# Decoder step on one core: samples in two groups of four with streamed keys, query tiles in another order

## What is computed

```
s_c = qg . kc ;  p_c = masked_softmax(s_c)          # compressed blocks
score = sum of p_c over the head group, per block of 64 keys
_, idx = top_k(score, 16)                           # selected blocks
s_s = qg . k_sel ;  p_s = masked_softmax(s_s)       # keys of the selected blocks
s_w = qg . kw ;     p_w = masked_softmax(s_w)       # window of 512 keys
o = g0 * (p_c . vc) + g1 * (p_s . v_sel) + g2 * (p_w . vw)
```

## Time and profile before

| | us |
|---|---|
| median of 3 runs | 1167.39 |
| lowest and highest | 1166.18, 1168.58 |
| profiled execution | 1169.66 |
| its span | 1167.9 |
| granted TensorE clock over the span | 0.993 |

### The profile page before, as it was taken

How to read it: one execution, slowest core, us unless ns; L and a number is a source line. 1 busy time by engine, 2 the same in 40 slices (tenths; PEclk the granted TensorE clock), 3 DMA queues, 4 the chain that set the end, 5 groups by cost and what they waited for, 6 DMA issues and landing times.

```text
span 1167.9 us, 17973 instructions
## 1 busy us (share of the span) xinstructions
PE 1125.9 (96%) x7124; PEld 926.1 (79%) x7124; DVE 749.5 (64%) x1375; ACT 386.4 (33%) x822; POOL 360.5 (31%) x364
## 2 busy tenths in 40 slices
PE   6999999999999998999999999899999999998997
PEld 6888999999988855565656465688799999997884
DVE  3677889999974588665555556565655730266745
ACT  3202111123233666756555556401112121353000
POOL 3544520000003687573626345300022221317000
PEclk9999999999999999999999999999999999999999
DMA  7752512343220200231222211732131111041321
GB/s 234 241 164 108 181 36 55 90 170 109 51 41 1 95 25 1 74 116 66 90 92 73 109 35 75 179 127 72 43 112 36 54 36 44 17 145 72 127 90 45
DMA packets 81468, 103.18 MB, mean 88 GB/s; under 512 B 21632, under 2 KB 64776, under 8 KB 81311
## 3 DMA queue, kind: packets, MB, share of 16 engines
q1 hardware_dynamic: 69737, 67.41, 18.8%
q0 software_dynamic: 9472, 33.56, 8.3%
q10 hardware_dynamic: 2182, 1.16, 0.4%
HBM read 90.42 MB, written 16.64 MB: 92 GB/s over the span
## 4 chain that ended last, share of the span: by engine, by line
PE 85%; DVE 5%; DMA 3%; POOL 2%; ACT 2%; issue 2%; SPq 0%; DVEq 0%; ACTq 0%
PE PS L697 24%; PE PS L1682 16%; PE PS L1860 15%; PE PS L1222 6%; PE PS L1208 6%; PE PS L1097 6%; PE PS L685 3%; PE PS L1135 2%; PE PS L1140 2%; DMA WRAW<-in_w_in_even 2%; PE PS L1181 1%; DVE ACC L557 1%; PE PS L1840 1%; DMA WOR<-in_w_out_even 1%; DVE XL L2034 1%
## 5 line engine op out<-in xcount | busy, mean ns | idle before, releaser
L604 DVE SCALAR_TENSOR_TENSOR Y<-U,SM,Y 128x1024 f32<-128x1024 f32 x120 | 147.9, 1293 | 0.3
L697 PE MATMUL PS<-XH,WH 128*128 128x352 f32 (+1 forms) x648 | 147.0, 331 | 0.0
L697 PE MATMUL PS<-XL,WH 128*128 128x352 f32 (+1 forms) x648 | 144.1, 327 | 0.0
L697 PE MATMUL PS<-XH,WL 128*128 128x352 f32 (+1 forms) x648 | 143.3, 325 | 0.0
L697 PEld LDWEIGHTS PS<-XH,WH 128*128 128x128 f32 (+1 forms) x648 | 107.9, 186 | 2.7
L697 PEld LDWEIGHTS PS<-XH,WL 128*128 128x128 f32 (+1 forms) x648 | 108.2, 185 | 1.4
L697 PEld LDWEIGHTS PS<-XL,WH 128*128 128x128 f32 (+1 forms) x648 | 108.0, 186 | 1.4
L1967 POOL TENSOR_TENSOR WL<-WRAW,WH 128x1024 fp32r<-128x1024 f32 x14 | 37.8, 2701 | 217.8 <-ACT WH L1912 217.8
L557 DVE SCALAR_TENSOR_TENSOR ACC<-PS,SM,ACC 128x508 f32<-128x508 f32 x124 | 86.9, 742 | 25.2 <-PE PS L685 23.1
L288 POOL TENSOR_TENSOR WL<-WRAW,WH 128x1024 fp32r<-128x1024 f32 x12 | 28.7, 2390 | 233.1 <-ACT WH L361 233.1
L1682 PE MATMUL PS<-WOH,XH 128*128 128x512 f32 (+1 forms) x288 | 92.2, 402 | 6.1 <-DVE GT L2029 3.1
(11 more groups left out here) (315 smaller groups left out, 2099.6 us busy)
## 6 DMA issues: line engine op xcount, KB each, us to landing
WRAW<-in_w_in_even SPq DMA_DIRECT2D x16, 512.0 KB, 3.9
WRAW<-in_w_in_odd SPq DMA_DIRECT2D x16, 512.0 KB, 4.0
XIN<-in_x_prompt SPq DMA_DIRECT2D x8, 512.0 KB, 13.4
WRAW<-in_w_in_even SPq DMA_DIRECT2D x16, 256.0 KB, 3.7
TM<-in_state_win_kv SPq DMA_DIRECT2D x8, 512.0 KB, 8.8
XR<-in_x_prompt SPq DMA_DIRECT2D x8, 512.0 KB, 3.6
layer_out<-R SPq DMA_DIRECT2D x8, 512.0 KB, 2.6
XR<-layer_out SPq DMA_DIRECT2D x8, 512.0 KB, 3.4
```

The lines of the kernel that those rows point to most:

```text
L604: v.scalar_tensor_tensor(dst, src, CWT[:, i, t:t + 1], dst, ALU.mult, ALU.add).then_inc(s_cv, 1)
L697: ins = pe.matmul(PS[0:mcols, 3 * slot + c, 0:CH], w[:, slot, kk, 0:mcols], x[:, kk, c * CH:(c + 1) * CH], start=(kk == 0 and n == 0), sto ...
```

## The change

1. **Two groups of four samples** instead of four groups of two. A group takes all 128 partitions. RING, of the same size, has room for 2 quarters of 4 samples. Quarters are streamed: keys 0 and 1 are gathered, quarter 2 when the last key turn of quarter 0 is done, quarter 3 likewise behind quarter 1. The products run in 6 parts: quarters 2 and 3, which are there, then the window of samples 2 and 3 of the group and the new tokens, then quarters 0 and 1, gathered a second time (behind parts 0 and 1), then the window of samples 0 and 1, loaded a second time. So there are 6 gathers of four samples per group, 48 DMAs instead of 32, and 12 window loads instead of 8.
2. The window scores of samples 0 and 1 come first in a group, those of 2 and 3 behind quarter 2. They are still scored two at a time (`scw`).
3. Score blocks of the cached keys hold four samples (four strips of 32 columns, 4 KTS tiles). Turns of probabilities are of 128 by 128, five fills of four and one of two. Turned probabilities lie in four places (`turned`).
4. The planner's numbers: a gather of four is 5000 ns, key turns are due 6000 ns after it; parts 3 and 4 of the products likewise. `RANK_LAG`, the distance between ranks, goes from 200 to 1000 ns. DVE's priority goes from PRMOQXHW to PRMOQHXW.
5. Query tiles in the order 3, 2, 1, 0, 4 to 7.
6. SP loads the output weights behind parts 3 and 4 of the second group; the loads of windows wait by `sp_windows_again`.

The diff, cut to its core:

```diff
-            sp_windows(sp, range(2))
+            sp_windows(sp, 0)
-        UNITS = [(qt, gp, br) for qt in (2, 1, 0, 3, 4, 5, 6, 7) for gp in range(2) for br in (SELBR, WINB, CMPB)]
+        UNITS = [(qt, gp, br) for qt in (3, 2, 1, 0, 4, 5, 6, 7) for gp in range(2) for br in (SELBR, WINB, CMPB)]
-        RING = at("RING", [P, 4, 2, 1024], F32, 126720)
-        KTS = at("KTS", [P, 2, 512], F32, 114048)
+        RING = at("RING", [P, 2, 4, 1024], F32, 126720)
+        KTS = [at(f"KTS{i}", [P, 512], F32, o) for i, o in enumerate((114048, 116096, 101376, 103424))]
-        PV_PARTS = 5
+        PV_PARTS = 6
-        RANK_LAG = 200
+        RANK_LAG = 1000
-        for i in range(2):
-            step("POOL", "X", ("gather", 0, i), 2500)
+        step("POOL", "X", ("gather", 0, 0), 5000)
         step("POOL", "X", ("prep",), 3300)
-        for i in range(2, 4):
-            step("POOL", "X", ("gather", 0, i), 2500, ("H", 3))
+        step("POOL", "X", ("gather", 0, 1), 5000, ("H", 3))
...
+        for a in range(2):
+            four = range(4 * a, 4 * a + 4)
+
+            def key_tile(b, i):
+                fill(("kt", b, i), 520, ("late", ("gather", a, i), 6000) if i < 4 else None)
+                take("ACT", ("kt", b, i), 600, ("rank", 1, 5))
+
+            def window_scores(pair):
+                for b in four[2 * pair:2 * pair + 2]:
+                    key_tile(b, 4)
+                fill(("scw", a, pair), 1000)
+                take("DVE", ("scw", a, pair), 920)
+
+            window_scores(0)
+            for i in range(4):
+                for b in four:
+                    key_tile(b, i)
+                if i < 2:
+                    step("POOL", "X", ("gather", a, i + 2), 5000, ("kt", four[3], i))
+                fill(("sc", a, i), 1100)
+                take("DVE", ("sc", a, i), 770)
+                if i == 2:
+                    window_scores(1)
...
+            for i in range(6):
+                fill(("pt", a, i), 550 if i < 5 else 250, ("sscale", a, i // 4))
+                take("ACT", ("pt", a, i), 600)
             for k in range(PV_PARTS):
+                fill(("pv", a, k), (1150, 950, 1400, 950, 950, 950)[k], ("late", ("gather", a, k + 1), 6000) if k in (3, 4) else None)
                 bank7[0] = None
+                if k < 2:
+                    step("POOL", "X", ("gather", a, 4 + k), 5000, ("pv", a, k))
+                if k in (3, 4) and a == 0:
+                    step("POOL", "X", ("gather", 1, k - 3), 5000, ("pv", a, k))
...
-        URGENT = {"PE": "SXTVY", "DVE": "PRMOQXHW", "ACT": "PXEW", "POOL": "CXAW"}
+        URGENT = {"PE": "SXTVY", "DVE": "PRMOQHXW", "ACT": "PXEW", "POOL": "CXAW"}
...
+                    b0 = 4 * x[1] + (2 * x[2] if x[0] == "scw" else 0)
+                    for b in range(b0, b0 + (2 if x[0] == "scw" else 4)):
+                        ins = pe.matmul(PS[rows_of(b), 7, :], QBD[:, b, :], KTS[b % 4][:, :], start=True, stop=True)
...
+                    if part in (3, 4):
+                        pe.wait_ge(s_ring[part - 3], 64 * (3 * a + 3))
+                    if part == 5:
+                        for i in range(2):
+                            pe.wait_ge(s_wc[i], 16 * (3 * a + 3))
+                    four = range(4 * a, 4 * a + 4)
+                    quarter = {0: 2, 1: 3, 3: 0, 4: 1}.get(part)
...
+        def sp_windows_again(sp):
+            for a in range(2):
+                sp.wait_ge(s_xf, bank7_filled(("kt", 4 * a + 1, 4)))
+                sp_windows(sp, 2 * a + 1)
+                sp.wait_ge(s_pvq, 5 * a + 3)
+                sp_windows(sp, 2 * a)
+                if a == 0:
+                    sp.wait_ge(s_pvb, 1)
+                    sp_windows(sp, 2)
...
-                        sp.wait_ge(s_pvq, 14 + kk // 2)
+                        sp.wait_ge(s_pvq, 9 + kk // 2)
-                sp.wait_ge(s_pvq, 16)
-            sp_windows(sp, range(2, DB))
+            sp_windows_again(sp)
```

More of the change, by code:

```diff
@@ L995, in program @@
                      ("late", ("rank", a, n - 1) if n else ("rank", 0, 5), RANK_LAG) if a or n else None)
[L996 to L1005, removed]
+        for a in range(2):
[18 more added lines that the diff above has]
+                    window_scores(1)
+            fill(("new", a), 500)
+            take("DVE", ("new", a), 550)
+            step("DVE", "X", ("low", a), 330)
@@ L1006, in program @@
             for k in range(3):
-                step("ACT", "X", ("sexp", gi, k), 1100 if k < 2 else 920, ("low", gi))
-            step("DVE", "X", ("srec", gi), 400, ("sexp", gi, 2))
+                step("ACT", "X", ("sexp", a, k), 1100 if k < 2 else 920, ("low", a))
+            step("DVE", "X", ("srec", a), 400, ("sexp", a, 2))
             for k in range(2):
[L1010 to L1013, removed]
+                step("POOL", "X", ("sscale", a, k), 810 if k else 2080, ("srec", a))
@@ L1019, in program @@
[L1019 to L1022, removed]
+                if k < 2:
+                    step("POOL", "X", ("gather", a, 4 + k), 5000, ("pv", a, k))
+                if k in (3, 4) and a == 0:
+                    step("POOL", "X", ("gather", 1, k - 3), 5000, ("pv", a, k))
+            take("DVE", ("pv", a, PV_PARTS - 1), 250)
+            fill(("ot", a), 200)
+            take("DVE", ("ot", a), 450)
@@ new lines, in sample @@
+                    quarter = {0: 2, 1: 3, 3: 0, 4: 1}.get(part)
+                    terms = [(22, b) for b in four] if part == 0 else []
+                    if quarter is not None:
+                        terms += [(n, b) for n in range(4 * quarter, 4 * quarter + 4) for b in four]
+                    elif part == 2:
+                        terms += [(n, b) for n in range(16, 20) for b in four[2:]] + [(n, b) for n in (20, 21) for b in four]
+                    else:
+                        terms += [(n, b) for n in range(16, 20) for b in four[:2]]
@@ new lines, in sample @@
+                    for n, b in terms:
+                        c0 = 32 * (b % 4)
+                        if n < 16:
+                            v0 = n % 4 * 256 + P
+                            w = RING[:, n // 4 % 2, b % 4, v0:v0 + P]
+                        elif n < 20:
+                            w = window(b)[:, n - 16, P:256]
+                        if n < 20:
+                            p = turned(n, 1)[:, 0, c0:c0 + 32]
+                        elif n < 22:
+                            v0 = 384 + 256 * (n - 20)
+                            p, w = PTN[:, n - 20, c0:c0 + 32], TM[0:NSAMP, 8, v0:v0 + P]
+                        else:
+                            p, w = PTC[0:NCS, b // 4, rows_of(b)], VCN[0:NCS, b, :]
+                        ins = pe.matmul(PS[rows_of(b), 7, 0:P], p, w, start=(n == 22), stop=(n == (19 if b in four[:2] else 7)))
@@ L1186, in sample @@
+                    ins.then_inc(s_pvb if part == PV_PARTS - 1 else s_pvq, 1)
                 elif x[0] == "ot":
@@ L1356, in sample @@
                 elif x[0] == "srec":
[L1357 removed]
                     v.wait_ge(s_eex, 3 * x[1] + 3)
[L1359 to L1361 removed]
+                    link(v.tensor_tensor(EDN[:, 2:3], EDN[:, 2:3], EDN2[:, :], ALU.add))
+                    v.reciprocal(ERC[:, 2:4], EDN[:, 2:4]).then_inc(s_ern, 1)
+                elif x[0] == "take":
```

175 lines of the change are left out of this document (76 added, 99 removed).

## The result

The changed kernel takes 1154.38 us (median of 4 runs, 1153.95 to 1155.27), beside 1166.99 us for the kernel before on the same chip: a ratio of 0.9891, with a 95% interval of 0.9877 to 0.9905. The profiled execution took 1155.27 us with a span of 1153.5, against 1169.66 and 1167.9.

A forecast was written before the change was run, and what follows sets the result against it. The prediction took a full PE to bound the middle of the attention stage. Work minus 16.8, start minus 3, window plus 7.7 and late loads plus 2 gave minus 10.1 us: 1157.3 us from 1167.4, range 1148 to 1169.

The forecast's parts named there:

- Scores and products: Sample blocks on PE: four strips run at once, so score blocks save 7.9 us and value products 8.4 us.
- Rival (c): Sample blocks on PE: four strips don't run at once, products and scores cost as now, 1174 us; chance 0.03.
- Turns: Turns of probabilities on PE: from 7.0 us to twice 6.5 us a group, minus 0.5 us.
- rival (d): Middle of attention: PE not quite full, half of 16.8 us becomes waiting for DVE or POOL, 1166 us; chance 0.15.
- The window wait: Second group's first window load: PE stands 6 us, then a low clock costs 1.7 us, together plus 7.7.
- Late loads: Twelve fills in attention wait for loads asked for shortly before: plus 2 us for all, ends 0 and 20.
- Rival (a): PE's in-order waits for twelve late loads add up; gain gone at 12 us, 1175 us at 20; chance 0.07.
- The start: Start of attention: tile 3 first and wider-spaced ranks feed PE better, minus 3 us, ends minus 8 and plus 5.
- The chain: Serial sample work beside the prompt: starts near 468 us, ends at 683, 24 us to spare, so not the bound.
- rival (b): The serial sample chain becomes the bound, setting the end from 24 us late; 1173 us at 40 late; chance 0.05.
- The end: End of attention: the stage ends near 721 us and everything behind it shifts alike.

The follow-up runs named there:

- second pair: The changed kernel and the kernel before, both run again unchanged on another chip: ratio 0.9900; the kernel before took 1164.29 us in a single execution.
- tiles_2103: The changed kernel with only the old query tile order 2, 1, 0, 3 put back: 1169.71 us, 1.0019 times the kernel before.
- group_only: The changed kernel with old tile order, old rank distance and old DVE priority, keeping the grouping of four: 1179.86 us, 1.0025 times the kernel before on a slower chip.
- before_again: The kernel before, unchanged, profiled on another chip that turned out like the first: 1164.29 us, a single execution.
- old_ranks: The changed kernel with the old rank distance and ranks ahead of XL put back, tile 3 still first: 1175.00 us, 1.0077 times the kernel before.
- window_later: The changed kernel with the second group's first window scores moved behind quarter 0: 1177.08 us, 1.0004 times the kernel before on a slower chip.
- scores_twice: The changed kernel with every sample score matmul issued twice, same result: 1173.70 us, 0.9968 times the kernel before on a slower chip.

## Why the prediction was right, and where it was not

The forecast was 1157.3 us, the measurement 1154.38, and the mechanism forecast, less work on a full PE, is what the traces show. Point by point:

**Scores and products (minus 7.9, minus 8.4).** Measured by starts: minus 7.7 and minus 8.5. That four strips run at once was read from one block of another kind, and held to the hundredth: 0.99 us a block, 0.25 a term. Rival (c) falls. The Trainium skill ("TensorE: Matmul & The Clock Gate", Part 3, The mechanism) has LDWEIGHTS overlap matmuls in flight only where the row groups differ; the eight records of a term share theirs and still go in 0.25 us, so here the measurement decides against it.

**Turns (minus 0.5).** Turns and new scores together gave minus 1.6. With what the prompt's blocks gained from new neighbours, which the sum did not have, the work fell by 19.0 instead of 16.8.

**PE is full (rival (d)).** It falls: PE's waits for DVE, ACT and POOL in the stage are 8.8 us before and 8.9 after (8.4 and 9.1 in the second pair), where (d) had them grow by 8, and doubled scores show in the time.

**The window wait (plus 7.7).** It came where it was named, near the middle, and the low clock behind it too. It was 2.7 us by the wait, plus 1.7 for 3.4 us of lower clock: some 4.5, and 4.0 in the second pair (2.3 and 1.7). PE was ready for the key turn 2.7 us after the load's issue at 579.29, close to the 2.5 forecast. But the load landed after 5.2 us, not 8.8, and sooner than the shortest in the earlier trace rows, 6.7. This is the term that was too large.

**Late loads (plus 2).** 2.2 us of waits for RING against 0.2 before, with the gathers landing in 4.4 to 9.7 us, median 5.7. Rival (a) falls for this kernel; in tiles_2103 it is half true, 5.6 us.

**The start (minus 3).** Minus 3.3 in the first pair, plus 1.2 in the second. The size was a guess and no run supports it; with the lower clock taken off as above, it is minus 1.4 and minus 2.4.

**The chain (start 468, end 683).** It started at 476.6 and ended at 693.3. Its own length, 216.7 us, was forecast at 215; only its start was off. The ranks and XL alone bring it to 468.4 (tiles_2103), as forecast, against 459.1 in group_only; the new tile order, which the working did not count here, adds the other 8. The chain was not the bound, and rival (b) falls. But between its end and the stage's there were 20.7 us, where the forecast had 38, of which the output weights take 14.

**The end (stage near 721, all behind it moves alike).** The stage ended at 714, 17.4 us earlier. But what lies behind grew by 2.9 us, a step that failed. PE's waits for WOL are 3.0 us as before, but in one piece:

```profile
728.18 1.22 PE L1730 MATMUL PS<-WOH,XH 128*128 128x512 f32 x2 [2.96 <-POOL WOL L1714]
```

In the kernel before they were two pieces of 1.7 and 1.3 with no lower clock behind them. Here the clock is at its lower level for 3.4 us from 728 and 6.8 us from 1042, 3.4 us more lost behind the stage than before.

**The sum in the first pair.** Work minus 19.0, loss plus 3.0 (window 4.5, late loads 2.0, start minus 3.3, and minus 0.2 that has no name), behind the stage plus 2.9: minus 13.1. The stage also began 1.5 us earlier, which the change does not explain, since before_again begins there too; with it the span's 14.4 are accounted for to 0.2. That minus 10.1 came so near is partly luck: the window was 3.2 us too large, the work 2.2 too small, and the growth behind the stage was not in the sum.

**What the working lacked.** It put the change down as terms that add up, and gave the plan none. The order of all engines is planned anew for every edit, and kernels that had the same work removed came out between 0.989 and 1.008. tiles_2103, old_ranks and window_later are each one to three lines from the changed kernel; two lie at or above the upper end of the range and all above the kernel before or level with it. What undid the 19 us in them is named above (projection ahead of value blocks, late loads, lower clock, and on slower chips PE's late counts), but not priced: no run took one away without bringing another. None of it could be read from the trace of before. So the sum was right about the work and right by half an accident about the loss: 6.7 forecast (7.7, 2 and minus 3), 3.0 and 7.4 in the two pairs.

## What to carry to other kernels

Cost work on a full, in-order engine from start to start, and use one block of the trace that already has the new shape: that gave two terms to within 0.2 us. But where a planner makes the order, an edit is also a new draw of the order, here worth 1 to 2%: look at the new order before believing a sum (what now stands ahead of the last blocks, how many gathers go in a row, which load is asked for last), and test an edit in more than one order before crediting it. Do not credit the removal of a wait with the wait's length: in three kernels here the wait went and the gain expected of it did not come, though on other chips than the changed kernel's. And where a wait is put down to nobody, look at what its semaphore counts before guessing.

## What was not expected of the hardware

Two kinds of chip. The kernel before took 1167 us on two and 1176 to 1177 on three. A part goes with the granted clock, 0.997 on the even chip and 0.990 to 0.992 on the slower ones (medians of its executions). At 0.993 to 0.994 its span is 1165.2 to 1168.0 on the first and the even chip and 1171.7 to 1174.0 on the slower ones, so some 6 us remain. Behind the stage the profiles of both kinds agree (436 to 440 us), so the difference is likely to lie in the attention stage. Only the slower chips show counts of PE that reach ACT and DVE late: stops of 0.7 to 3.0 us beside short rows of gathers, 12.8 us beside eight in a row. The kernel before has such a row of eight, so a part of the time that the slower chips' ratios are taken against may be this stall. That isn't shown, since it was not profiled there.

In the changed kernel a wait of PE of 2.7 and one of 3.0 us in one piece each came with 3.4 us of lower clock, while the two of 1.7 and 1.3 us in the kernel before, 4.4 us apart, did not. PE's waits for POOL's WOL repeat this in all profiles. In the seven with one piece, of 2.9 to 8.3 us, the clock was at its lower level there for 3.4 to 10.2 us; in six with two pieces of 1.3 to 1.7 us it was not. scores_twice, with pieces of 1.3 and 1.8 us and one of 0.6 for DVE between them, had 3.4 us of it.
